# A two-block sequence model in float32 on one core: operands moved to one common place modulo 512 bytes, and the split weights of eight-tile units set 16, 32, 64 and 256 bytes into their buffers

## The chip, the core and the metric

The kernel runs on one core of a Trainium2 chip. The metric is device microseconds of one execution, as the median of several runs; lower is better. Engines are named as the profile names them: PE multiplies matrices and loads its weights (PEld), ACT, DVE and POOL work elementwise, SP issues the transfers from memory.

## The reference, cut to what matters

Two blocks over 512 frames of 1024 channels, float32. Every block is a chain of a normalisation, a wide projection, a mixer (delta rule and state space heads, then stick-breaking attention with pooling, then gated linear attention), a projection back, and a convolutional feed-forward layer of width 2816. What takes the time is the products of the activations with the weights:

```python
proj = h @ w_in                                  # 1024 x (mixer width)
mix = jnp.concatenate([o_a, o_s], axis=-1) @ w_out
u = causal_dwconv(h @ w_up, ffn_conv_w, ffn_conv_b)   # 1024 x 5632, three times
gate, up = jnp.split(u, 2, axis=-1)
f = (jax.nn.silu(gate) * up) @ w_down                 # 2816 x 1024, three times
```

Nothing of this arithmetic is touched by the change.

## The kernel before, in words

**Products.** Activations lie with channels on the 128 partitions and the 512 frames along a row, so a tile of activations is 128 x 512 words, 2048 bytes in every partition. A weight unit is one output tile of 128 channels: eight (or eleven, in the down projections) blocks of 128 x 128 words, 512 bytes each in every partition. Each product is made in fp32r, a faster matmul form, from a high and a low part of both operands: for each block k there are three matmuls, high weight by high activations, high weight by low activations, low weight by high activations (`multiply`, lines 253 to 255, 24 of them for a unit of eight tiles and 33 for one of eleven). `fan` (lines 229 to 231) does the same for the first two or three units of a stage side by side, and `mix_pe` (lines 2632 to 2634) for the first mixer's projection back. Every matmul has a weight load of its own, which the profile shows as PEld beside the matmul before it.

**Buffers.** SP loads a unit into one of four `raw` buffers (`load_units`). ACT writes the rounded high part to `whi[u % 2]` (`split_hi`, line 185) and DVE the rest to `wlo[u % 2]` (`split_lo`, line 191). Both wait for semaphores of the unit two places before. So units alternate between two pairs of buffers. `first_weights` (`first_hi`, `first_lo`) are two more pairs in the scratch region for the first two units of a stage, and `early` two for the first stage of all.

**Where things lie.** `fixed` hands out rows one behind the other, each rounded up to 32 bytes: `X`, `HH` and `HL` (the high and low part of the normalised activations, eight tiles each), four `raw`, two `whi`, two `wlo` (5632 bytes each), then `par` (914 columns of parameters), `cst` and `small`. Behind them, at the next multiple of `LINE` = 128 bytes, `FREE` begins, the scratch region, whose parts stand at multiples of 2048 bytes from `FREE`: the high and low parts that the feed-forward layer makes (`FH`, `FL`, 22 tiles each), those of the mixers' outputs (`DH`/`DL`, `MH`/`ML`, `PH`/`PL`), the `first` and `early` weights, and the mixers' own scratch. `TMP`, six more tiles, is counted from the end of the memory.

All rows up to `par` are multiples of 512 bytes long, and `X` is put at byte 16512, so `X`, `HH`, `HL`, `raw`, `whi` and `wlo` all begin at 128 modulo 512. `par` takes 3656 bytes, rounded up 3680, which is 7 x 512 + 96; `cst` and `small` are multiples of 512. So `FREE` falls on 224 rounded up to 256 modulo 512: everything in scratch stands 128 bytes on from everything in front of `par`, modulo 512. A block of weights is 512 bytes and a tile 2048, so within a buffer every block and every tile begins at the same place modulo 512 as the buffer.

**Order of the work.** The stages follow one another as in the reference; PE takes units in their order, `acc` alternates between two accumulators, and ACT, DVE and POOL handle a unit's results while PE is at the next ones. In the feed-forward layers PE runs 44 units of eight tiles on `HH`/`HL` (up) and then 16 units of eleven tiles on `FH`/`FL` (down), three times over. In the mixers, units are run in parts of six matmuls between the mixer's own small ones.

Of the kernel before, what the change touches and what calls it, by code (L numbers as in the profile page):

```python
# [25 lines left out]
P = 128  # L26
S = 512
D = 1024
KD = D // P
# [4 lines left out]
LINE = 128  # L34
RAW = 4
SPLIT = 2
# [3 lines left out]
def at(base, i, per):  # L40

    return base if i is None else base + per * i
# [22 lines left out]
def program(nc, x_in, w8, w11, par_in, cst_in, small_in, out, plan):  # L65
    cols = columns()
    ctx = ExitStack()
    with ctx:

        top = [(nc.sbuf_base + 31) // 32 * 32]  # L70

        def fixed(name, shape, dt=F32):
            t = nc.alloc_sbuf_tensor_at(name, shape, dt, offset=top[0])
            top[0] += (4 * shape[1] + 31) // 32 * 32
            return t

        X = fixed("X", [P, KD * S])
        base_h = top[0]
        HH = fixed("HH", [P, KD * S], F32R)
# [2 lines left out]
        raw = [fixed(f"raw{j}", [P, HALF * P]) for j in range(RAW)]  # L82
        whi = [fixed(f"whi{j}", [P, HALF * P], F32R) for j in range(SPLIT)]
        wlo = [fixed(f"wlo{j}", [P, HALF * P], F32R) for j in range(SPLIT)]
        par = fixed("par", [P, cols.n])
        cst = fixed("cst", [P, 15 * P])
        small = fixed("small", [P, small_in.shape[1]])
        FREE = (top[0] + LINE - 1) // LINE * LINE
        TMP = (nc.sbuf_usable_end - 6 * TILE) // LINE * LINE

        def place(name, n, offset, dt=F32):
            assert offset >= FREE and offset + 4 * n <= nc.sbuf_usable_end, name
            return nc.alloc_sbuf_tensor_at(name, [P, n], dt, offset=offset)
# [19 lines left out]

        sq = [place(f"sq{j}", S, TMP + j * TILE) for j in range(2)]
        hn = [place(f"hn{j}", S, TMP + (2 + j) * TILE) for j in range(2)]
        ln = place("ln", S, TMP + 4 * TILE)
        rs = place("rs", S, TMP + 5 * TILE)
        squares = place("squares", KD * S, FREE + 24 * TILE)
        taps = [place(f"taps{j}", S, TMP + j * TILE) for j in range(4)]
        FH = place("FH", KF * S, FREE, F32R)  # L120
        FL = place("FL", KF * S, FREE + KF * TILE, F32R)
        assert FREE + 2 * KF * TILE <= TMP
        first_weights = {}
        for at0 in (0, 8, 16):
            first_weights[at0] = [tuple(place(f"first_{n}{at0}_{j}", KD * P, FREE + (at0 + 4 * j + 2 * m) * TILE, F32R)
                                        for m, n in enumerate(("hi", "lo"))) for j in range(2)]
# [51 lines left out]

        def split_hi(act, u, i, per, kt, first=None, behind=SPLIT):

            hi = whi[u % SPLIT] if first is None else first[0]
            act.wait_ge(raw_in[u % RAW], at(16 * (u // RAW + 1), i, 16 * per // RAW))
            if u >= behind and first is None:
                act.wait_ge(unit_done, at(u - behind + 1, i, per))
            nc.scalar.activation(hi[:, 0:kt * P], raw[u % RAW][:, 0:kt * P], ACT.Copy).then_inc(w_hi_ready, 1)  # L185

        def split_lo(dve, u, i, per, kt, first=None, behind=SPLIT):

            hi, lo = (whi[u % SPLIT], wlo[u % SPLIT]) if first is None else first
            dve.wait_ge(w_hi_ready, at(u + 1, i, per))  # L190
            nc.vector.tensor_tensor(lo[:, 0:kt * P], raw[u % RAW][:, 0:kt * P],  # L191
                                    hi[:, 0:kt * P].bitcast(F32), ALU.subtract).then_inc(w_lo_ready, 1)
# [27 lines left out]
        def fan(pe, c, hi, lo, ready, after=None):  # L220

            u0, n = c["u"], c["fan"]
            w = [c["first"][j] if j < 2 else (whi[(u0 + j) % SPLIT], wlo[(u0 + j) % SPLIT]) for j in range(n)]
            pe.wait_ge(w_lo_ready, u0 + n)
            for k in range(KD):
                pe.wait_ge(ready[0], ready[1] + k + 1)
                for j in range(n):
                    a, (wh, wl) = c["spare"][j], (x[:, k * P:(k + 1) * P] for x in w[j])
                    nc.tensor.matmul(a[:, :], wh, tile(hi, k), start=k == 0, stop=False)  # L229
                    nc.tensor.matmul(a[:, :], wh, tile(lo, k), start=False, stop=False)  # L230
                    last = nc.tensor.matmul(a[:, :], wl, tile(hi, k), start=False, stop=k == KD - 1)  # L231
                    if k == KD - 1:
                        last.then_inc(unit_done, 1)
                if after and k in after:
                    after[k]()

        def multiply(pe, u, t, i, per, per_t, kt, hi, lo, start=True, stop=True, ready=None, part=None, c=None):

            w, a, m = u % SPLIT, acc[t % 2], None
            if c and u - c["u"] < len(c["spare"]) + 2:  # L240
                m = u - c["u"]
                a = accum(c, m)
            if not part:
                pe.wait_ge(w_lo_ready, at(u + 1, i, per))
                if m is not None:
                    pe.wait_ge(acc_read, c["t"])
                elif start and t >= 2:
                    pe.wait_ge(acc_read, at(t - 1, i, per_t))
            for k in range(kt) if part is None else range(kt * part // 4, kt * (part + 1) // 4):
                if ready:  # L250
                    pe.wait_ge(ready[0], ready[1] + k + 1)
                wh, wl = whi[w][:, k * P:(k + 1) * P], wlo[w][:, k * P:(k + 1) * P]
                nc.tensor.matmul(a[:, :], wh, tile(hi, k), start=start and k == 0, stop=False)  # L253
                nc.tensor.matmul(a[:, :], wh, tile(lo, k), start=False, stop=False)  # L254
                last = nc.tensor.matmul(a[:, :], wl, tile(hi, k), start=False, stop=stop and k == kt - 1)  # L255
            if part in (None, 3):
                last.then_inc(unit_done, 1)
# [23 lines left out]
        def norm_act(act, c, made):  # L281
            for k in range(KD):
                act.wait_ge(*made(k))
                square(act, c, tile(X, k), k, sq, hn[0])
            split_hi(act, 0, None, 0, KD, early[0])
# [8 lines left out]
        def norm_dve(dve, c, gain):  # L294
# [8 lines left out]
            for k in range(KD + 1):  # L303
                if k < KD:
                    nc.vector.scalar_tensor_tensor(out=tile(normed_x, k), in0=tile(X, k), scalar=col(gain[0], gain[1] + k),
                                                   in1=rs[:, :], op0=ALU.mult, op1=ALU.mult).then_inc(hn_ready, 1)
# [10 lines left out]
        def later_act(act, c, gain, made):  # L317
            for k in range(KD):
                act.wait_ge(*made(k))
                nc.scalar.activation(tile(HH, k), tile(X, k), ACT.Copy, scale=col(gain[0], gain[1] + k)).then_inc(hh_ready, 1)  # L320
                nc.scalar.activation(tile(squares, k), tile(X, k), ACT.Square).then_inc(sq_ready, 1)
            next_splits(split_hi, act, c["next"])
# [4 lines left out]
        def ahead_act(act, c, gain, made, k):  # L327
            act.wait_ge(*made(k))
            nc.scalar.activation(tile(HH, k), tile(X, k), ACT.Copy, scale=col(gain[0], gain[1] + k)).then_inc(hh_ready, 1)
            square(act, c, tile(X, k), k, sq, hn[0])  # L330

# [2289 lines left out]
        def mix_pe(pe, c):  # L2621
            for m, (k, h) in enumerate(MIX):
                u, w, a = c["u"] + m, (c["u"] + m) % SPLIT, mix_acc(c, k)
                pe.wait_ge(w_lo_ready, u + 1)
                if h == 0 and k not in (2, 3):
                    pe.wait_ge(acc_read, c["t"] + k - 1)
                hi, lo = ((DH, DL), (HH, HL))[h]
                for j in range(KD):
                    if m in (0, 4):
                        pe.wait_ge(h_ready, c["h"] - 2 * KD + h * KD + j + 1)  # L2630
                    wh, wl = whi[w][:, j * P:(j + 1) * P], wlo[w][:, j * P:(j + 1) * P]
                    nc.tensor.matmul(a[:, :], wh, tile(hi, j), start=h == 0 and j == 0, stop=False)  # L2632
                    nc.tensor.matmul(a[:, :], wh, tile(lo, j), start=False, stop=False)  # L2633
                    last = nc.tensor.matmul(a[:, :], wl, tile(hi, j), start=False, stop=h == 1 and j == KD - 1)  # L2634
                last.then_inc(unit_done, 1)
                if m == 1:
                    ssd_sums(pe, 1)
                if m == len(MIX) - 2:
                    squares_pe(pe, c, total1)
            last_square_pe(pe, c, sq1)  # L2640
# [36 lines left out]
        n = dict(next_first=None, u=-1, t=0, sq=0, rms=0, hn=0, h=0, ffn=0, pair=0, scaled=0, ssum=0, add=0, hh=0, tap=0, conv=0, x=0, w8=0, w11=0)  # L2677
# [4 lines left out]
        for at_, (kind, arg) in enumerate(plan):  # L2682
            c = dict(n)
# [293 lines left out]
```

## Time and profile before

| | |
|---|---|
| runs, us | 2166.68, 2168.47, 2169.84; median 2168.47 |
| profiled execution, first to last instruction | 2157.8 us (what its run took around that is not listed; the median of the runs is 10.7 us above it) |
| PE busy | 2109.7 us, 98% |
| PEld busy | 1698.0 us, 79% |
| DVE, ACT, POOL busy | 1213.1, 906.3, 325.6 us |
| granted clock of PE, mean | 0.998 |
| DMA | 88 GB/s in the mean |

The busy time of PE counts a matmul from its start to the modelled end of its pass through the array, and matmuls overlap, so the busy share says little about the rate. The rate is the distance from the start of one matmul to the start of the next.

### The profile page before, as it was taken

The numbers are of one execution on the slowest core, as the hardware profiler recorded it, in microseconds if no ns is written. First come the engines' busy times: TensorE is split into PE (matmuls) and PEld (weight loads), VectorE is DVE, ScalarE is ACT, GpSimd is POOL, SyncE is SP. The second block draws the span as 40 slices with busy tenths as digits, with TensorE's granted clock in tenths as the row PEclk, the third lists the DMA queues.
The fourth block names the chain that finished last, engine by engine and source line by source line (L and its number), as shares of the span: only waits on it lengthen the run. The fifth ranks groups of instructions, "written<-read, shape, count | busy, mean of one in ns | idle before, by whom it ended". The sixth has DMA issues, their size and how long they took to land.

```text
span 2157.8 us, 26841 instructions
## 1 busy us (share of the span) xinstructions
PE 2109.7 (98%) x9776; PEld 1698.0 (79%) x9776; DVE 1213.1 (56%) x1663; ACT 906.3 (42%) x1282; POOL 325.6 (15%) x266
## 2 busy tenths in 40 slices
PE   6999999999999999999999999999999999999999
PEld 5778888878868888877766888888878878888887
DVE  5898755765366665226544566653354465666522
ACT  6883445434254444224564444442242354444311
POOL 0002121220122222001302122210000011222100
PEclk9999999999999999999999999999999999999999
DMA  7323322122323233221111333232222122323321
GB/s 234 93 77 92 86 74 69 59 69 69 101 65 97 94 94 120 94 86 59 59 40 50 97 94 94 95 116 96 80 77 88 51 78 88 98 97 97 114 94 66
DMA packets 81481, 188.96 MB, mean 88 GB/s; under 512 B 19824, under 2 KB 40432, under 8 KB 81392
## 3 DMA queue, kind: packets, MB, share of 16 engines
q1 hardware_dynamic: 81392, 187.75, 27.6%
q8 instruction: 59, 0.97, 0.2%
q14 instruction: 30, 0.25, 0.0%
HBM read 178.28 MB, written 9.44 MB: 87 GB/s over the span
## 4 chain that ended last, share of the span: by engine, by line
PE 92%; DVE 4%; ACT 2%; issue 1%; DMA 0%; POOL 0%; SPq 0%; ACTq 0%; DVEq 0%; POOLq 0%
PE acc L253 23%; PE acc L255 23%; PE acc L254 23%; PE bank L1726 1%; PE bank L1245 1%; PE bank L229 1%; PE bank L230 1%; PE bank L231 1%; PE acc L2634 1%; PE acc L2633 1%; PE acc L2632 1%; PE bank L2017 1%; PE bank L253 1%; PE bank L255 1%; PE bank L254 1%
## 5 line engine op out<-in xcount | busy, mean ns | idle before, releaser
L253 PE MATMUL acc<-HH,whi 128*128 128x512 f32 x1600 | 642.1, 401 | 7.1 <-DVE wlo L191 4.5
L255 PE MATMUL acc<-HH,wlo 128*128 128x512 f32 x1600 | 624.4, 390 | 0.0
L254 PE MATMUL acc<-HL,whi 128*128 128x512 f32 x1600 | 623.5, 390 | 0.0
L185 ACT ACTIVATE whi<-raw 128x1024 fp32r<-128x1024 f32 (+1 forms) x293 | 324.2, 1108 | 573.5 <-PE acc L255 543.4
L191 DVE TENSOR_TENSOR wlo<-raw,whi 128x1024 fp32r<-128x1024 f32 (+1 forms) x293 | 400.9, 1369 | 287.8 <-ACT whi L185 287.8
L253 PEld LDWEIGHTS acc<-HH,whi 128*128 128x128 f32 x1600 | 301.1, 188 | 74.1 <-DVE wlo L191 11.0
L255 PEld LDWEIGHTS acc<-HH,wlo 128*128 128x128 f32 x1600 | 300.5, 188 | 64.0
L254 PEld LDWEIGHTS acc<-HL,whi 128*128 128x128 f32 x1600 | 301.1, 188 | 62.0 <-issue 4.1
L253 PE MATMUL acc<-FH,whi 128*128 128x512 f32 x528 | 208.9, 396 | 0.0
L255 PE MATMUL acc<-FH,wlo 128*128 128x512 f32 x528 | 208.6, 395 | 0.0
L254 PE MATMUL acc<-FL,whi 128*128 128x512 f32 x528 | 208.5, 395 | 0.0
L388 DVE TENSOR_TENSOR acc<-acc,rs 128x512 f32<-128x512 f32 x150 | 104.8, 699 | 174.8 <-PE acc L255 174.8
L480 POOL TENSOR_TENSOR taps<-taps,taps 128x512 f32<-128x512 f32 x66 | 85.5, 1295 | 507.1 <-DVE taps L466 451.3
L445 ACT ACTIVATE FH<-taps 128x512 f32 (+1 forms) x66 | 41.8, 633 | 199.1 <-POOL taps L480 199.1
L253 PEld LDWEIGHTS acc<-FH,whi 128*128 128x128 f32 x528 | 99.1, 188 | 24.2 <-issue 0.2
L254 PEld LDWEIGHTS acc<-FL,whi 128*128 128x128 f32 x528 | 99.1, 188 | 24.2 <-issue 0.2
L255 PEld LDWEIGHTS acc<-FH,wlo 128*128 128x128 f32 x528 | 99.1, 188 | 24.1
L343 POOL TENSOR_TENSOR hn<-hn,sq 128x512 f32<-128x512 f32 x24 | 36.8, 1532 | 418.6 <-ACT sq L336 418.6
L466 DVE SCALAR_TENSOR_TENSOR taps<-acc,par,taps 128x510 f32<-128x510 f32 x117 | 87.6, 749 | 14.7 <-DVE taps L462 0.5
L485 POOL TENSOR_TENSOR FL<-taps,FH 128x512 f32 (+1 forms) x66 | 85.6, 1297 | 59.9 <-ACT FH L445 59.9
L436 ACT ACTIVATE taps<-acc,par 128x512 f32<-128x512 f32 x117 | 89.1, 762 | 1.6 <-DVE acc L388 1.6
L462 DVE SCALAR_TENSOR_TENSOR taps<-acc,par,taps 128x511 f32<-128x511 f32 x117 | 86.7, 741 | 0.0
(394 smaller groups left out, 2673.1 us busy)
## 6 DMA issues: line engine op xcount, KB each, us to landing
raw<-w SPq DMA_DIRECT2D x257, 512.0 KB, 3.5
raw<-w SPq DMA_DIRECT2D x48, 704.0 KB, 4.0
X<-x SPq DMA_DIRECT2D x4, 512.0 KB, 5.2
x_dram<-small SPq DMA_DIRECT2D x8, 256.0 KB, 4.4
xt_dram<-small SPq DMA_DIRECT2D x8, 256.0 KB, 3.6
a_dram<-l_am SPq DMA_DIRECT2D x8, 256.0 KB, 3.7
l_xt<-xt_dram SPq DMA_DIRECT2D x8, 256.0 KB, 3.5
l_x<-x_dram SPq DMA_DIRECT2D x8, 256.0 KB, 3.3
```

The source lines that it names most:

```text
L185: nc.scalar.activation(hi[:, 0:kt * P], raw[u % RAW][:, 0:kt * P], ACT.Copy).then_inc(w_hi_ready, 1)
L191: nc.vector.tensor_tensor(lo[:, 0:kt * P], raw[u % RAW][:, 0:kt * P], hi[:, 0:kt * P].bitcast(F32), ALU.subtract).then_inc(w_lo_ready, 1)
L253: nc.tensor.matmul(a[:, :], wh, tile(hi, k), start=start and k == 0, stop=False)
L254: nc.tensor.matmul(a[:, :], wh, tile(lo, k), start=False, stop=False)
L255: last = nc.tensor.matmul(a[:, :], wl, tile(hi, k), start=False, stop=stop and k == kt - 1)
L388: nc.vector.tensor_tensor(a[:, :], a[:, :], rs[:, :], ALU.mult).then_inc(scaled, 1)
L436: nc.scalar.activation(taps[j][:, :], a[:, :], ACT.Identity, scale=w(2), bias=w(3)).then_inc(tap_ready, 1)
L445: nc.scalar.activation(o, taps[j - 1][:, :], ACT.Copy).then_inc(fh_ready, 1)
L462: nc.vector.scalar_tensor_tensor(out=taps[j][:, 1:S], in0=a[:, 0:S - 1], scalar=w(1), in1=taps[j][:, 1:S], op0=ALU.mult, op1=ALU.add).then ...
L466: nc.vector.scalar_tensor_tensor(out=taps[j][:, 2:S], in0=a[:, 0:S - 2], scalar=w(0), in1=taps[j][:, 2:S], op0=ALU.mult, op1=ALU.add).then ...
L480: nc.gpsimd.tensor_tensor(taps[2 * b][:, :], taps[2 * b][:, :], taps[2 * b + 1][:, :], ALU.mult).then_inc(prod_ready, 1)
L485: nc.gpsimd.tensor_tensor(o, taps[2 * b][:, :], h.bitcast(F32), ALU.subtract).then_inc(f_ready, 1)
```

## The change

`par` moves to the front, and what follows it is rounded up to a multiple of 128 bytes. All later rows are multiples of 512 bytes long, so `X`, `HH`, `HL`, `raw`, `whi`, `wlo`, `cst`, `small` and `FREE` now begin at the same place modulo 512 (an assertion says so of `FREE`). Further, a new helper `weights` gives the high and low part of a unit: for units of eleven tiles they begin at the start of the buffers, as before; for units of eight tiles they begin 4 words (16 bytes) into `whi[0]`, 8 words (32 bytes) into `wlo[0]`, 16 words (64 bytes) into `whi[1]` and 64 words (256 bytes) into `wlo[1]`. ACT's and DVE's splits write there, and `fan`, `multiply` and `mix_pe` read there. The `first` and `early` weights are not shifted. No instruction is added or removed, and no wait is changed.

```diff
+        par = fixed("par", [P, cols.n])
+        top[0] = (top[0] + LINE - 1) // LINE * LINE
         X = fixed("X", [P, KD * S])
...
-        par = fixed("par", [P, cols.n])
+        SHIFT = ((4, 8), (16, 64))
+
+        def weights(w, kt):
+
+            hi, lo = SHIFT[w] if kt == KD else (0, 0)
+            return whi[w][:, hi:hi + kt * P], wlo[w][:, lo:lo + kt * P]
+
         cst = fixed("cst", [P, 15 * P])
...
         FREE = (top[0] + LINE - 1) // LINE * LINE
+        assert (FREE - base_h) % S == 0
...
-            hi = whi[u % SPLIT] if first is None else first[0]
+            hi = weights(u % SPLIT, kt)[0] if first is None else first[0]
...
-            hi, lo = (whi[u % SPLIT], wlo[u % SPLIT]) if first is None else first
+            hi, lo = weights(u % SPLIT, kt) if first is None else first
...
-            w = [c["first"][j] if j < 2 else (whi[(u0 + j) % SPLIT], wlo[(u0 + j) % SPLIT]) for j in range(n)]
+            w = [c["first"][j] if j < 2 else weights((u0 + j) % SPLIT, KD) for j in range(n)]
...
-                wh, wl = whi[w][:, k * P:(k + 1) * P], wlo[w][:, k * P:(k + 1) * P]
+                wh, wl = (x[:, k * P:(k + 1) * P] for x in weights(w, kt))
...
-                    wh, wl = whi[w][:, j * P:(j + 1) * P], wlo[w][:, j * P:(j + 1) * P]
+                    wh, wl = (x[:, j * P:(j + 1) * P] for x in weights(w, KD))
```

## Rows read from the trace of the kernel before

**Rows 1.** The page: span and busy time of the engines.

```profile
span 2157.8 us, 26841 instructions
...
PE 2109.7 (98%) x9776; PEld 1698.0 (79%) x9776; DVE 1213.1 (56%) x1663; ACT 906.3 (42%) x1282; POOL 325.6 (15%) x266
```

**Rows 2.** The page: the chain that ended last, shares of the span by engine.

```profile
PE 92%; DVE 4%; ACT 2%; issue 1%; DMA 0%; POOL 0%; SPq 0%; ACTq 0%; DVEq 0%; POOLq 0%
```

**Rows 3.** Busy time by window, PE alone, up projections: stretch, length, busy (matmuls), clock, DMA.

```profile
660.00:840.00 180.00, 180.00 (x796) 1.00 0.31 99
1240.00:1450.00 210.00, 210.00 (x927) 1.00 0.32 102
```

**Rows 4.** The same view of stretches in two down projections.

```profile
895.00:955.00 60.00, 60.00 (x259) 1.00 0.27 87
1475.00:1565.00 90.00, 90.00 (x387) 1.00 0.26 85
```

**Rows 5.** Timeline of PE (start, length), fan of the second up stage, 33 matmuls.

```profile
1560.83 0.39 PE L229 MATMUL bank<-HH,first_hi 128*128 128x512 f32 x1
...
1568.30 0.39 PE L231 MATMUL bank<-HH,first_lo 128*128 128x512 f32 x1
```

**Rows 6.** Timeline of PE, last projection back: first and last of 43 matmuls.

```profile
1759.83 0.39 PE L253 MATMUL acc<-PH,whi 128*128 128x512 f32 x1
...
1769.59 0.39 PE L253 MATMUL acc<-PH,whi 128*128 128x512 f32 x1
```

**Rows 7.** Lines 218 and 254: matmul durations in ns, min/median/max.

```profile
L218 PE MATMUL bank<-first_hi x36: 387/389/792, 594.4 to 977.7; 128*128 128x512 f32 x36
...
L254 PE MATMUL acc<-HL,whi x1600: 387/389/628, 34.0 to 2030.9; 128*128 128x512 f32 x178
...
L254 PE MATMUL acc<-FL,whi x528: 387/392/404, 848.3 to 2154.0; 128*128 128x512 f32 x176
```

**Rows 8.** Timeline of PE while the granted clock is at its lower level.

```profile
1748.41 0.50 PE L253 MATMUL acc<-PH,whi 128*128 128x512 f32 x1 [2.73 <-DVE PL L764]
...
1749.79 0.63 PE L255 MATMUL acc<-PH,wlo 128*128 128x512 f32 x1
...
1752.35 0.63 PE L255 MATMUL acc<-PH,wlo 128*128 128x512 f32 x1
```

**Rows 9.** Timeline of PE, one part of a unit between small matmuls, first mixer.

```profile
194.77 0.39 PE L254 MATMUL acc<-HL,whi 128*128 128x512 f32 x1
...
195.93 0.38 PE L2084 MATMUL bank<-l_qd,l_small 128*128 128x128 f32 x2
```

**Rows 10.** Groups by line and shape, PE: count, busy us, mean ns, idle before.

```profile
L253 PE MATMUL acc<-HH,whi 128*128 128x512 f32 x1600 | 642.1, 401 | 7.1 <-DVE wlo L191 4.5 <-ACT l_z L1793 2.4
...
L253 PE MATMUL acc<-FH,whi 128*128 128x512 f32 x528 | 208.9, 396 | 0.0
...
L253 PE MATMUL bank<-HH,whi 128*128 128x512 f32 x88 | 36.5, 414 | 0.0
L229 PE MATMUL bank<-HH,first_hi 128*128 128x512 f32 x80 | 34.4, 429 | 1.0 <-DVE HL L361 1.0
...
L253 PE MATMUL acc<-MH,whi 128*128 128x512 f32 x64 | 26.1, 408 | 1.6 <-DVE wlo L191 1.1 <-POOL ML L1182 0.5
...
L253 PE MATMUL acc<-PH,whi 128*128 128x512 f32 x64 | 25.9, 405 | 2.7 <-DVE PL L764 2.7
...
L2632 PE MATMUL acc<-HH,whi 128*128 128x512 f32 x48 | 19.1, 398 | 0.0
L2632 PE MATMUL acc<-DH,whi 128*128 128x512 f32 x48 | 19.0, 396 | 0.0
...
L2632 PE MATMUL bank<-DH,whi 128*128 128x512 f32 x16 | 6.7, 419 | 0.0
```

**Rows 11.** The same view, ACT: the high parts of units of eight tiles.

```profile
L185 ACT ACTIVATE whi<-raw 128x1024 fp32r<-128x1024 f32 x245 | 257.9, 1054 | 371.7 <-PE acc L255 341.6 <-PE acc L2634 12.4 <-PE bank L231 8.7
```

**Rows 12.** The same view, DVE: the low parts of units of eight tiles.

```profile
L191 DVE TENSOR_TENSOR wlo<-raw,whi 128x1024 fp32r<-128x1024 f32 x245 | 322.9, 1319 | 155.6 <-ACT whi L185 155.6
```

## The prediction, made before the changed kernel was run

> **What bounds the kernel now.** The page comes first: PE is busy for 98% of the span, DVE for 56%, ACT for 42% [rows 1], and the chain that ended last runs through PE for 92% of its length and through DMA for none [rows 2]. So PE's rate sets the time almost everywhere, and whatever changes the distance between two matmuls is paid in full. Busy time doesn't show that distance, since matmuls overlap; I read it from how many fit into a stretch. The view of busy time by window counts every matmul that runs in it, so also the one that began up to 0.39 us (its length) ahead. In two up projections that is 180.39 us / 796 = 226.6 ns and 210.39 / 927 = 227.0 ns [rows 3]; I use 226.7. In two down projections it is 60.39 / 259 = 233.2 ns and 90.39 / 387 = 233.6 ns [rows 4]; I use 233.4. Both stretches are filled by matmuls of one shape, at the full granted clock, with no idle time.
>
> Why do the down projections go 6.7 ns slower? In the up projections weights (`whi`, `wlo`) and activations (`HH`, `HL`) begin at the same place modulo 512. In the down projections the activations (`FH`, `FL`) stand 128 bytes further than the weights. Two other pairs tell whether that is it or something in the down projections. In a fan, `HH` meets weights of the scratch region, so that now the weights stand 128 bytes further: 32 matmuls lie between the starts of the two rows, 7.47 us / 32 = 233.4 ns [rows 5]. In the last projection back `PH` meets `whi` and `wlo`: 42 matmuls in 9.76 us, 232.4 ns [rows 6]. And where line 218 multiplies scratch by scratch, the median duration is 389 ns, as for `HL` by `whi`, where `FL` by `whi` has 392 [rows 7]. So neither the region nor the stage decides, but whether both operands stand at the same place. Also, the extra time isn't a fixed price of a matmul: while the granted clock is at its lower level of 1.2 GHz, after PE had sat idle for 2.73 us, six matmuls of the 128-byte pair take 2.56 us, 426.7 ns each, which is 512 columns at 1.2 GHz with nothing on top [rows 8]. At 2.4 GHz 512 columns would be 213.3 ns, so the same place costs 13.4 ns on top and 128 bytes apart 20.1 ns.
>
> **The change, part by part.** A matmul's own weights are loaded while the one before runs, so the distance that counts is between a running tile and the next block of weights.
>
> (a) `FH` and `FL` come to the place of the unshifted weights: 528 x 3 = 1584 matmuls [rows 10] by 233.4 - 226.7 = 6.7 ns, 10.6 us off.
>
> (b) `first` weights come to the place of `HH` and are not shifted: 80 x 3 = 240 matmuls [rows 10] by 6.7 ns, 1.6 us off.
>
> (c) The units of eight tiles on `HH` and `HL` lose the common place that they had: (1600 + 88 + 48) x 3 = 5208 matmuls [rows 10]. The trace has no row of 16, 32, 64 or 256 bytes. Bounds: from below, all of the 13.4 ns goes, since at 512 columns and 2.4 GHz nothing is left to gain; from above, the nearest slower row is 233.4 ns, 6.7 ns more. I take the straight line between the two distances that have rows, 6.7 / 128 = 0.052 ns a byte: 0.8 ns for 16 bytes, 1.7 for 32, 3.4 for 64. For 256 bytes I take nothing: +128 and -128 cost the same [rows 4, 5], and those are one place only if the pattern repeats every 256 bytes. Two of every three loads are of the high part, so units in the first pair of buffers pay (2 x 0.8 + 1.7) / 3 = 1.1 ns and those in the second (2 x 3.4 + 0) / 3 = 2.3 ns, 1.7 in the mean: 5208 x 1.7 = 8.9 us on.
>
> (d) `DH`, `MH`, `PH` and their low parts go from 128 bytes to the shifts: (48 + 16 + 64 + 64) x 3 = 576 matmuls [rows 10] by 6.7 - 1.7 = 5.0 ns, 2.9 us off.
>
> (e) ACT's and DVE's splits write at shifted addresses. They take 1054 and 1319 ns and have 371.7 us of PE-made idle time and 155.6 us of ACT-made idle time ahead of them [rows 11, 12]: that idle time hides a longer split, and I cost it at nothing. Were the cover gone, the end of it would show where PE waits for `wlo`, 4.5 us in all in the largest group [rows 10]; a fifth longer there would be 1 us. Moving `par` changes no issue and no queue.
>
> Sum: -10.6 - 1.6 + 8.9 - 2.9 = -6.2 us. Against the profiled span that is 2157.8 to 2151.6; the median of the runs stands 10.7 us above that span, for what lies around it, and goes to 2162. Not all of (c) is settled at 226.7 today: in the short parts between a mixer's small matmuls five distances at the common place took 1.16 us, 232 ns each [rows 9], so the place is not all that counts there. The first mixer has 53 units, 1272 matmuls; if they feel nothing of the shift, (c) is 2.2 us cheaper.
>
> **The rivals.** With x for the mean price of the shifts per matmul, the whole is -12.2 - 3.9 + 5.78 x us (5784 matmuls of units of eight tiles); it turns from gain to loss at x = 2.8 ns.
>
> *The shift breaks what the common place gave* (slower). The up projections hold 226.7 ns over hundreds of matmuls [rows 3], while at the same place short parts run at 232 [rows 9]. So 226.7 may be a state that the stream falls into and keeps, and every unit now changes the distance, twice within itself. Then all units of eight tiles run as `FH` does today: x = 6.7, +22.7 us, 2191. For it: no stretch in which the operands stand apart goes under 232.4 [rows 4 to 6]. Against: 16 and 32 bytes are small beside 128. It shows first in the up projections, and decides from a period of 229.5 ns on. Chance 0.36, with everything past x = 3.5.
>
> *The shift pays.* If the common place is itself a collision of the two reads, a few bytes could part them. Half of the 13.4 ns regained, x = -6.7, is -54.9 us: 2114. For it: the 13.4 ns are there to be had [rows 3, 8]. Against: no stretch shown goes under 226.6. Chance 0.12.
>
> *The place does nothing*, and what parts 226.7 from 233.4 is something else, or gains and losses cancel: 2168. Against: rows 5 to 7 exchange stage and region and keep the 6.7 ns. The Trainium skill, TensorE: Matmul & The Clock Gate, section "Step-by-step: what each phase is for", says that PE reads moving tiles and weights through two independent ports and that loading the next weights takes nothing from the running matmul; by that rule the change is worth 0 and the time stays at 2168. The two periods, 226.7 and 233.4 ns for one shape, do not agree with it. Chance 0.1.
>
> **How the numbers follow.** A measurement of this kernel tells 0.2%, 4.3 us, from no change. My forecast, the line between the rows with x from about -1 to 3, has 0.42; its own range is 2146 to 2170, its middle 2162. Of it 0.35 lie below x = 2.0, where the gain passes 4.3 us. Faster: 0.35 + 0.12 = 0.47; within 0.2%: 0.07 + 0.1 = 0.17; slower: 0.36. The range reaches to just past the slower rival at 2191, and a third of the way to the gain at full rate: 2136 to 2193.
>
> **What would show it.** In the profile after: down projections at 226.7 ns and `FL` by `whi` at a median of 389 (part a); fans of `first` weights at 226.7 (b); in the up projections alternate units of different period, the first pair of buffers near 227.8 and the second near 229.0 (c); DMA, ACT and DVE as they are (e). The forecast is wrong if the up projections run at 231 or more, or under 226, and its ground is wrong if the down projections stay at 233.

## The result, and the profile after

| | before | after |
|---|---|---|
| median of the runs, us | 2166.83 (6 runs, 2158.72 to 2169.84) | 2177.49 (6 runs, 2176.16 to 2178.87) |
| ratio, with its 95% interval | | 1.0058 [1.0040, 1.0076] |

The changed kernel is slower by 10.7 us in the medians, 12.6 us by the ratio. Its profiled execution took 2178.87 us for a span of 2177.1, so 1.8 us lie around a span, and not the 10.7 us that the prediction put there: the rest goes with the granted clock. The span is 19.3 us above that of [rows 1], more than the medians differ, because the profiled execution of before was one of the quicker ones (mean granted clock 0.998, after it 0.995): its trace has the clock at the lower level for 10 us of the span, the trace after for 24 us. So I take sizes from medians and ratios, and from the traces only what doesn't depend on that: the distance between matmuls inside a stage at full clock.

The medians still mix executions of different clock. Of those that have 0.997, the kernel before took 2161.0 to 2161.8 us (four, among those measured beside the experiments), the changed one 2176.2 (one): at the same clock the change costs about 15 us.

The page of the kernel after, its span, its engines and the chain that ended last (compare [rows 1, 2]):

```profile
span 2177.1 us, 26841 instructions
...
PE 2131.1 (98%) x9776; PEld 1705.2 (78%) x9776; DVE 1212.1 (56%) x1663; ACT 905.7 (42%) x1282; POOL 325.6 (15%) x266
...
PE 91%; DVE 5%; ACT 2%; issue 1%; DMA 0%; POOL 0%; DVEq 0%; ACTq 0%
```

The same instructions ran, with the same engine in charge. DVE, ACT and POOL are as busy as before to 1 us; only PE has more to do.

Busy time by window for PE of the kernel after, two up projections and one down projection (stretch, length, busy with the count of matmuls, clock, DMA share, GB/s; compare [rows 3, 4]):

```profile
660.00:840.00 180.00, 180.00 (x773) 1.00 0.29 93
1240.00:1450.00 210.00, 210.00 (x902) 1.00 0.31 99
900.00:950.00 50.00, 50.00 (x222) 1.00 0.27 94
```

Counted as in the prediction (the stretch and 0.39 us, over the count) the up projections now run at 180.39 / 773 = 233.4 ns and 210.39 / 902 = 233.2 ns, where they had 226.7, and the down projection at 50.39 / 222 = 227.0 ns, where it had 233.4. The two kinds of stage have changed places, and there are about twice as many matmuls in the slower kind.

Timeline of PE of the kernel after, in the first up projection (start, length): two starts with 27 distances between them, a whole unit of eight tiles and the beginning of the next, from the other pair of buffers:

```profile
694.96 0.40 PE L262 MATMUL acc<-HH,whi 128*128 128x512 f32 x1
...
701.26 0.40 PE L262 MATMUL acc<-HH,whi 128*128 128x512 f32 x1
...
1574.97 0.39 PE L238 MATMUL bank<-HH,first_hi 128*128 128x512 f32 x1
...
1579.73 0.39 PE L238 MATMUL bank<-HH,first_hi 128*128 128x512 f32 x1
```

6.30 / 27 = 233.3 ns across both pairs: the pair with 16 and 32 bytes isn't cheaper than the one with 64 and 256 (over the whole projection, unit by unit, 233.4 and 233.3). The last two rows are a fan of unshifted `first` weights, 21 distances in 4.76 us, 226.7 ns, where it had 233.4 [rows 5]. (In both kernels this fan opens the third mixer, not an up stage: it follows the second down projection.)

Line 263 (it was 254) of the kernel after, durations of its matmuls in ns as min/median/max (compare [rows 7]):

```profile
L263 PE MATMUL acc<-HL,whi x1600: 387/394/628, 32.9 to 2053.6; 128*128 128x512 f32 x178
L263 PE MATMUL acc<-FL,whi x528: 389/389/398, 863.9 to 2173.3; 128*128 128x512 f32 x176
...
L263 PE MATMUL acc<-ML,whi x64: 390/394/398, 1142.3 to 1207.0; 128*128 128x512 f32 x64
```

Groups by line and shape of the kernel after; lines 262, 194 and 200 were 253, 185 and 191 (busy us, mean ns, idle before; compare [rows 10 to 12]):

```profile
L262 PE MATMUL acc<-HH,whi 128*128 128x512 f32 x1600 | 653.8, 409 | 6.4 <-DVE wlo L200 3.9 <-ACT l_z L1802 2.3
...
L194 ACT ACTIVATE whi<-raw 128x1024 fp32r<-128x1024 f32 x245 | 257.7, 1053 | 394.2 <-PE acc L264 363.9 <-PE acc L2643 12.4 <-PE bank L240 8.7
L200 DVE TENSOR_TENSOR wlo<-raw,whi 128x1024 fp32r<-128x1024 f32 x245 | 322.9, 1319 | 147.9 <-ACT whi L194 147.9
```

`HL` by `whi` went from a median of 389 to 394 ns and `FL` by `whi` from 392 to 389. The splits take 1053 and 1319 ns, as before, and PE waits 3.9 us for `wlo` where it waited 4.5.

### The profile page after: what moved, and what is told of

Same layout as the page of the kernel before. It is cut to its first block, busy times and chain, and to the rows that moved or that the text cites. A ratio compares the mean times of both kernels' runs of the same rounds, so it can differ in the third digit from the quotient of the medians.

```text
span 2177.1 us, 26841 instructions
## 1 busy us (share of the span) xinstructions
PE 2131.1 (98%) x9776; PEld 1705.2 (78%) x9776; DVE 1212.1 (56%) x1663; ACT 905.7 (42%) x1282; POOL 325.6 (15%) x266
## 3 DMA queue, kind: packets, MB, share of 16 engines
q1 hardware_dynamic: 81392, 187.75, 27.1%
## 4 chain that ended last, share of the span: by engine, by line
PE 91%; DVE 5%; ACT 2%; issue 1%; DMA 0%; POOL 0%; DVEq 0%; ACTq 0%
PE acc L262 23%; PE acc L264 23%; PE acc L263 23%; PE bank L1254 1%; PE bank L238 1%; PE acc L2641 1%; PE acc L2643 1%; PE acc L2642 1%; PE bank L239 1%; PE bank L240 1%; PE bank L1735 1%; PE bank L2026 1%; DVE wlo L200 1%; PE bank L262 1%; PE bank L264 1%
## 5 line engine op out<-in xcount | busy, mean ns | idle before, releaser
L262 PE MATMUL acc<-HH,whi 128*128 128x512 f32 x1600 | 653.8, 409 | 6.4 <-DVE wlo L200 3.9
L264 PE MATMUL acc<-HH,wlo 128*128 128x512 f32 x1600 | 633.9, 396 | 0.0
L263 PE MATMUL acc<-HL,whi 128*128 128x512 f32 x1600 | 631.6, 395 | 0.0
```

## The experiments

Two theories stood against each other. **The line:** a distance between activations and weights costs in proportion to its bytes, up to 128. **The step:** any distance, however small, puts the stream into the slower period of 233 ns. Each run below also tells whether the two halves of the change, the moved rows and the shifts, add up.

In the runs called scans the rows lie as in the changed kernel, and each of the three up projections has shifts of its own, alike for the high and the low part unless it is said; all units elsewhere have none. Units alternate between two pairs of buffers, so one projection tells two distances. "Per unit" is the distance from the first matmul of a unit to the first of the next, over 24.

**1. The moved rows alone (align_only).** No shifts.

```diff
-        SHIFT = ((4, 8), (16, 64))
+        SHIFT = ((0, 0), (0, 0))
```

> The changed kernel with all four shifts at zero, so that every pair of weights and activations stands at one place modulo 512. All theories: units of eight tiles go back to 226.7 ns a matmul, the down projections stay at the 226.7 ns that they have after the change. Step theory (the shifts alone cost, 6.7 ns on each of the matmuls of the eight-tile units): the gains (a), (b) and (d) of the prediction remain, 12.2 + 3.9 = 16 us under the kernel before, near 2151 of 2167, ratio 0.9925. If the time were only 6 us under it, the gains were overrated by more than half; if not under it at all, the alignment buys nothing that the end sees.

Measured: 2147.96 us (2145.25 to 2153.03, 6 runs), before beside it 2167.26; ratio 0.991 [0.9895, 0.9924]. Windows of PE in this kernel:

```profile
660.00:840.00 180.00, 180.00 (x796) 1.00 0.30 98
1240.00:1450.00 210.00, 210.00 (x928) 1.00 0.32 101
900.00:950.00 50.00, 50.00 (x222) 1.00 0.27 85
```

Up and down projections alike run at 226.6 to 227.0 ns now. By the medians the moved rows gain 19.3 us, and the shifts cost 2177.5 - 2148.0 = 29.5 us, which is more than the whole loss of the change. At a mean granted clock of 0.997 three executions took 2145.3 to 2145.7 us, against 2161.0 to 2161.8 before: 15.8 us gained, and 30.7 lost by the shifts. So this kernel is quicker than both of the case.

**2. Equal shifts (scan_a).** The stage is looked up from the unit's number; the other scans change `SHIFT` alone. In words of 4 bytes, (high, low) of the first pair and of the second, for the three up projections:

```diff
-        SHIFT = ((4, 8), (16, 64))
+        SHIFT = (((4, 4), (8, 8)), ((16, 16), (32, 32)), ((64, 64), (48, 48)))
+        up_units = []
...
-        def weights(w, kt):
+        def weights(u, kt):
...
-            hi, lo = SHIFT[w] if kt == KD else (0, 0)
+            w = u % SPLIT
+            stage = [k for k, u0 in enumerate(up_units) if u0 <= u < u0 + 2 * KF]
+            hi, lo = SHIFT[stage[0]][w] if kt == KD and stage else (0, 0)
```

> High and low part of a unit shifted alike, other distances in each up projection, first and second pair of buffers: 16 and 32 bytes in the first, 64 and 128 in the second, 256 and 192 in the third; all other units unshifted. Line theory (the prediction's): 227.5 and 228.4 ns a matmul in the first, 230.0 and 233.4 in the second, 226.7 and 230.0 in the third. Step theory (every distance but a multiple of 256 bytes costs the same): 233.3 in the whole first and second, 226.7 in the units of 256 bytes. Mixture theory (it is only the change of the distance from load to load within a unit that costs): 226.7 in all but perhaps 128.

Measured: 2166.68 us. Windows of PE in three up projections:

```profile
660.00:840.00 180.00, 180.00 (x774) 1.00 0.30 94
1240.00:1450.00 210.00, 210.00 (x904) 1.00 0.31 100
1860.00:2020.00 160.00, 160.00 (x705) 1.00 0.31 96
```

That is 233.1 ns (16 and 32 bytes), 232.7 (64 and 128) and 227.5 (256 and 192). Per unit: 16 bytes 233.3, 32 bytes 232.8, 64 bytes 232.9, 128 bytes 232.4. The line asks for 227.5 at 16 bytes. The third projection holds two kinds of unit, as the timeline of PE shows, by the starts of a unit of 192 bytes, of one of 256, and of the next:

```profile
1921.58 0.39 PE L265 MATMUL acc<-HH,whi 128*128 128x512 f32 x1
...
1927.07 0.39 PE L265 MATMUL acc<-HH,whi 128*128 128x512 f32 x1
...
1932.51 0.39 PE L265 MATMUL acc<-HH,whi 128*128 128x512 f32 x1
```

5.49 / 24 = 228.8 ns at 192 bytes, 5.44 / 24 = 226.7 at 256. So 256 bytes is free, as the prediction took it, and the shifts from 16 to 128 bytes cost nearly the whole step. 192 bytes fits neither theory: the line asks for 230.0, the step for 233.3.

**3. Still smaller and larger shifts (scan_b).**

```diff
+        SHIFT = (((1, 1), (2, 2)), ((24, 24), (56, 56)), ((128, 128), (96, 96)))
```

> As the scan before it, with 4 and 8 bytes in the first up projection, 96 and 224 in the second, 512 and 384 in the third. Line theory: 226.9 and 227.1; 231.7 and 228.4 (32 bytes from 256); 226.7 and 233.4. Step theory: 233.3 in all but the units of 512 bytes, with 4 and 8 bytes open, since they stay within 16 bytes. If the pattern repeats every 512 bytes and not every 256, then 256 bytes cost something in the scan before and 512 nothing here. A stretch under 226.6 in either scan would speak for distances that pay.

Measured: 2167.64 us. Windows of PE, the same three stretches:

```profile
660.00:840.00 180.00, 180.00 (x779) 1.00 0.30 94
1240.00:1450.00 210.00, 210.00 (x901) 1.00 0.31 99
1860.00:2020.00 160.00, 160.00 (x697) 1.00 0.29 94
```

Per unit: 4 bytes 232.4, 8 bytes 231.0, 96 bytes 233.7, 224 bytes 233.3, 512 bytes 227.4, 384 bytes 232.9. One word of shift costs 5.7 of the 6.7 ns. And 384 bytes costs what 128 does while 512 is nearly free: the pattern repeats every 256 bytes.

**4. High and low part apart (scan_c).** One part shifted and the other not, then both off by distances that differ by 256 bytes; both pairs alike.

```diff
+        SHIFT = (((0, 16), (0, 16)), ((16, 0), (16, 0)), ((4, 68), (4, 68)))
```

> High and low parts at different distances, the same in both pairs of buffers: first up projection 0 for the high and 64 bytes for the low part, second 64 and 0, third 16 and 272. Line theory: a third, then two thirds of the price of 64 bytes (227.8 and 228.9 ns), third 227.5. Step theory with a price for every load off the common place: 228.9 with a third of the loads off it, 231.1 with two thirds, 233.3 with all. Mixture theory: the first two cost most, whatever the share, and the third, with 16 bytes for all loads modulo 256, costs nothing.

Measured: 2162.84 us. Windows of PE, the same three stretches:

```profile
660.00:840.00 180.00, 180.00 (x781) 1.00 0.30 95
1240.00:1450.00 210.00, 210.00 (x903) 1.00 0.31 100
1860.00:2020.00 160.00, 160.00 (x687) 1.00 0.29 94
```

That is 231.0 ns with only the low part 64 bytes off, 233.0 with only the high part, 233.5 with 16 and 272 bytes. Two of three loads are of the high part. One load off its place in three already costs 4.3 of the 6.7 ns, where a price per load would ask for a third of it, 2.2: the price belongs to the stream, not to the single load.

The third stretch begins too late to show the most telling thing of this run. Here are two windows of PE that cover the third projection from its start on, and the timeline between them:

```profile
1820.70:1858.60 37.90, 37.90 (x169) 1.00 0.32 100
1859.00:2037.00 178.00, 178.00 (x764) 1.00 0.30 98
```

```profile
1858.77 0.44 PE L265 MATMUL acc<-HH,whi 128*128 128x512 f32 x1
1859.05 0.39 PE L266 MATMUL acc<-HL,whi 128*128 128x512 f32 x1
```

With the same 16 and 272 bytes, seven units run at 38.29 / 169 = 226.6 ns. Then one distance is 0.28 us long, and from there to the end of the projection the pace is 178.39 / 764 = 233.5 ns. The kernel of the first experiment, without shifts, has a long distance (0.27 us) at the same unit, and comes back to its pace:

```profile
1816.00:1853.90 37.90, 37.90 (x169) 1.00 0.33 99
1856.20:2028.00 171.80, 171.80 (x759) 1.00 0.31 100
```

```profile
1854.05 0.44 PE L262 MATMUL acc<-HH,whi 128*128 128x512 f32 x1
1854.32 0.40 PE L263 MATMUL acc<-HL,whi 128*128 128x512 f32 x1
```

It has 226.6 ns ahead of it and 172.19 / 759 = 226.9 from nine matmuls behind it on. So one distance can hold either period. At the common place the stream came back after the disturbance, at 16 bytes modulo 256 it did not. The step theory is too simple in this, and the mixture theory, which expected no price here, was right for seven units.

**5. Shifts in whole multiples of 256 bytes (far_shift).** The split weights stand 256 and 256 bytes into the first pair, 512 and 768 into the second, in all units of eight tiles.

```diff
-        SHIFT = ((4, 8), (16, 64))
+        SHIFT = ((64, 64), (128, 192))
```

> All four buffers shifted, but by 256, 256, 512 and 768 bytes, the rest as changed. Step theory (only the place modulo 256 bytes counts): no price at all, 226.7 ns a matmul in the up projections, the time of the kernel with no shift, near 2148 (ratio 0.991 to the kernel before). If shifting as such costs (other addresses for the splits of ACT and DVE, other strides from buffer to buffer), or if the pattern is 512 bytes long, it is above 2155.

Measured: 2151.66 us (2150.80 to 2152.76, 4 runs), before beside it 2166.68; ratio 0.994 [0.9919, 0.9961]. Windows of PE:

```profile
660.00:840.00 180.00, 180.00 (x796) 1.00 0.31 98
1240.00:1450.00 210.00, 210.00 (x929) 1.00 0.32 102
```

226.6 and 226.5 ns, as without shifts. So shifting as such, the other addresses that ACT and DVE write and the places that PE reads, costs nothing to speak of; what costs is the place modulo 256. The median is 3.7 us above that of the first experiment, but all four executions had a clock of 0.993 (2150.8 to 2152.8 us), and the two of the first experiment at 0.993 took 2151.6 and 2153.0. That ACT and DVE write off the common place isn't what costs either: they did so throughout the seven units of the fourth experiment at 226.6 ns.

**6. Only one pair shifted (half_shift).**

```diff
-        SHIFT = ((4, 8), (16, 64))
+        SHIFT = ((4, 8), (0, 0))
```

> The changed kernel with the second pair of buffers unshifted, the first at 16 and 32 bytes. Step theory, with a stream that falls back into 226.7 ns within a unit: the units of the first pair at 233.3, those of the second at 227 to 228; half of the 29.5 us that lie between the changed kernel and the one without shifts, 2161 to 2165. If an unsettled stream stays unsettled, units of both pairs are near 233 and the time is near 2175. Line theory: 16 and 32 bytes are a third of the whole price, 2158.

Measured: 2164.28 us (2158.54 to 2170.32, 10 runs); ratio to before 0.9994 [0.9979, 1.0009]. A window of PE in the second up projection, then its timeline in the third: the start of an unshifted unit, of its tenth matmul, of the next (shifted) unit, and of the one after that:

```profile
1240.00:1450.00 210.00, 210.00 (x913) 1.00 0.31 100
```

```profile
1879.50 0.40 PE L262 MATMUL acc<-HH,whi 128*128 128x512 f32 x1
...
1881.58 0.39 PE L262 MATMUL acc<-HH,whi 128*128 128x512 f32 x1
...
1884.97 0.39 PE L262 MATMUL acc<-HH,whi 128*128 128x512 f32 x1
...
1890.56 0.40 PE L262 MATMUL acc<-HH,whi 128*128 128x512 f32 x1
```

The unshifted unit begins at 2.08 / 9 = 231.1 ns and goes on at 3.39 / 15 = 226.0, which is 226.7 within the rounding of the starts; the shifted one takes 5.59 / 24 = 232.9. A unit's pace follows its own place, but not at once: an unshifted unit needs some nine matmuls to come back to the quicker period. So half of the shifts lose somewhat more than half: 210.39 / 913 = 230.4 ns is 3.7 of the 6.7. The ratios agree (of the 1.48% between the first experiment's and the change's, 0.84%), but with intervals of 0.15% either way they wouldn't tell it from half. The time lies in the 2161 to 2165 expected of a stream that falls back within a unit.

**7. The shifts alone (shift_only).** The row order of before, with the change's shifts.

```diff
-        par = fixed("par", [P, cols.n])
-        top[0] = (top[0] + LINE - 1) // LINE * LINE
         X = fixed("X", [P, KD * S])
...
+        par = fixed("par", [P, cols.n])
         cst = fixed("cst", [P, 15 * P])
```

> The kernel before with the shifts alone, its rows where they were. Step theory: the matmuls on HH and HL go from 226.7 to 233.3 ns, as in the changed kernel, those on FH and FL stay at 233.4, those on the mixers' scratch stay near 233: the whole loss and none of the gain, 2167 + 29 = 2196, at most 2202 (5208 x 6.7 ns = 35 us). Line theory: 2176.

Measured: 2188.09 us (2185.44 to 2189.01, 4 runs); ratio 1.0107 [1.0085, 1.0130]. Windows of PE:

```profile
660.00:840.00 180.00, 180.00 (x773) 1.00 0.30 95
1240.00:1450.00 210.00, 210.00 (x902) 1.00 0.30 97
900.00:950.00 50.00, 50.00 (x216) 1.00 0.26 87
```

Up and down projections are both at 233.3 ns here. The shifts alone cost 21.4 us by the medians, 23.2 by the ratio; over the 5208 matmuls that leave their common place that is 4.1 to 4.5 ns each, and the sign of the change without its moved rows is beyond doubt. The step theory's 2196 is missed by 8 us: it charged every matmul the whole 6.7 ns, which the mixers don't pay (below). The halves add up only roughly: 29.5 us for the shifts behind the moved rows, less the 3.9 us of part (d), which the shifts alone can't undo, is 25.6, against these 21.4 to 23.2; what makes the difference stays open.

**8. Distances between 48 and 240 bytes (scan_d).**

```diff
+        SHIFT = (((60, 60), (52, 52)), ((44, 44), (40, 40)), ((36, 36), (12, 12)))
```

> Last scan of distances, high and low part alike, first and second pair of buffers: 240 and 208 bytes in the first up projection, 176 and 160 in the second, 144 and 48 in the third. Step theory: all between 231 and 234 ns, as 4 to 128 bytes were; distances short of 256 may be a little cheaper, as 192 bytes was (228.9). Collision theory (some place pays): a stretch under 226.6 ns somewhere; with none here, no distance in steps of 16 bytes up to 256 but 80 and 112 would be left for it.

Measured: 2162.37 us. Per unit: 240 bytes 227.8, 208 bytes 231.9, 176 bytes 230.3, 160 bytes 233.9, 48 bytes 233.1, and, against the rest, 144 bytes 226.9. Timeline of PE, third up projection, starts of a unit of 144 bytes, of one of 48, and of the next of 144:

```profile
1877.56 0.39 PE L265 MATMUL acc<-HH,whi 128*128 128x512 f32 x1
...
1883.00 0.40 PE L265 MATMUL acc<-HH,whi 128*128 128x512 f32 x1
...
1888.60 0.39 PE L265 MATMUL acc<-HH,whi 128*128 128x512 f32 x1
```

5.44 / 24 = 226.7 ns and 5.60 / 24 = 233.3. So some distances other than multiples of 256 reach the quicker period, but none tried goes under it.

**9. Two of these again, throughout a stage (scan_e).** 144 bytes in both pairs, 240 in both, and 80 and 112.

```diff
+        SHIFT = (((36, 36), (36, 36)), ((60, 60), (60, 60)), ((20, 20), (28, 28)))
```

> One distance for both pairs of buffers: 144 bytes in the first up projection and 240 in the second, the two distances between 0 and 256 at which units of the scan before held 226.7 ns; 80 and 112 bytes in the third, which no scan had. If the two are places of their own that hold the fast period, the first two stages run at 226.7 ns throughout, with no dearer matmul at the units' edges. If those units were only carried by their neighbours, they run at 231 to 234. For 80 and 112 bytes 231 to 234 is expected; under 226.6 would be a place that pays.

Measured: 2164.04 us. Windows of PE, the same three stretches as in the other scans:

```profile
660.00:840.00 180.00, 180.00 (x773) 1.00 0.30 95
1240.00:1450.00 210.00, 210.00 (x922) 1.00 0.32 101
1860.00:2020.00 160.00, 160.00 (x689) 1.00 0.30 96
```

144 bytes throughout runs at 233.4 ns, though it ran at 226.7 beside units of 48 bytes; 240 throughout runs at 228.2; 80 and 112 at 232.8. So the distance alone doesn't settle the period, as the third projection of the fourth experiment has shown already: what ran before a unit counts too. (The stage of 144 bytes alone began at the lower clock; whether it would hold 226.7 ns if it began at that pace wasn't tried.) The paces "per unit" of the scans hold beside the neighbours that they were measured with.

## Why the prediction was wrong

**What bounds the kernel: right.** PE's rate is the time. The matmul distances of the stages account for the direction of every run, and the other engines' busy times stayed.

**Parts (a) and (b): right.** Down projections came to 227.0 ns and the fans to 226.7, as forecast. With the shifts taken out, the moved rows gained 15.8 us at equal clock; the prediction's own formula at x = 0 has 16.1. The medians of the two kernels without any shift modulo 256 bytes lie on either side (19.3 us in the first experiment, 15.0 in the fifth).

**Part (c): the step that failed.** "I take the straight line between the two distances that have rows, 6.7 / 128 = 0.052 ns a byte". There is no line. Sixteen bytes cost 6.6 ns where the line has 0.8, 64 bytes 6.2 where it has 3.4, and 4 bytes 5.7; in the changed kernel both pairs of buffers run at 233.3 ns, where (c) had 227.8 and 229.0. What stands in its place is two periods, 226.7 and 233.3 ns: off the common place the stream can lose the quicker one at a single long distance and not come back (fourth experiment). The row that spoke against the line was there: [rows 3, 4] have two periods and nothing between, and [rows 9] show 232 ns at the common place itself, in short parts. Both say that 226.7 is something that the stream keeps only under conditions. The prediction saw this, and put it under its slower rival; as likeliest it took the interpolation, with nothing to show that the quantity is smooth.

**The size of it.** The whole change is 22.9 us worse than the -12.2 of (a) and (b), so -3.9 + 5.78 x = 22.9, and x = 4.6 ns a matmul; by the ratio (12.6 + 12.2 = 24.8) 5.0; at equal clock (14.9 + 12.2 = 27.1) 5.4. The forecast had 1.7 and the slower rival 6.7. In the up projections the rival is exact: 42 shifted units x 24 x 3 = 3024 matmuls by 6.7 ns are 20.3 us of the 29.5 that the shifts cost. The others, in the mixers and the projections back, bear the remaining 9.2 us: 2856 of them, 3.2 ns each (the count in (c) left out 96, two more groups of sixteen blocks, `bank<-HH,whi` at lines 229 and 2632; 0.2 us at its own price). The traces place them. From the last matmul of the first down projection to the first of the fan behind the second mixer, in the changed kernel and in the first experiment's:

```profile
984.04 0.39 PE L264 MATMUL acc<-FH,wlo 128*128 128x512 f32 x1
1207.42 0.39 PE L238 MATMUL bank<-HH,first_hi 128*128 128x512 f32 x1
...
975.19 0.39 PE L264 MATMUL acc<-FH,wlo 128*128 128x512 f32 x1
1196.35 0.39 PE L238 MATMUL bank<-HH,first_hi 128*128 128x512 f32 x1
```

223.4 us against 221.2, at the full clock throughout: 2.2 us over 528 shifted matmuls, 4.2 ns each. The stretch from the start to the fan behind the first mixer's projection back took 614.4 against 611.7 us, with 20 us at the lower clock in both: 2.7 us over 1593, 1.7 ns each. That its price is small fits [rows 9]: parts of six matmuls are over before the nine that an unshifted unit needed in the sixth experiment to settle. Over their last four distances the parts of six there (71 in each trace at the full clock) have a median of 231.5 ns without shifts and 232.3 with them, so there was little to lose; its units of 24 in a row go from 231.4 to 236.8.

**256 bytes at nothing: right** (226.7 ns in the second experiment, no loss in the fifth). The high part of that pair stood 64 bytes off, and the fourth experiment shows why a free low part then saves nothing: with only the high part off, 233.0 ns.

**Part (d): wrong with (c).** `ML` by `whi` has a median of 394 ns, no better than the 392 of a 128-byte pair [rows 7], since one off-place distance was exchanged for another of the same price. The 2.9 us were not there.

**Part (e): right.** The splits kept their durations to 1 ns, and the fifth experiment shifts them without a loss.

**The rivals.** *The shift breaks what the common place gave* is what happened, with its own sign shown by stage as it asked: up projections past 229.5 ns. Its 2191 is too high by the mixers' smaller price. *The shift pays* falls: of the distances tried, none held units under 226.6 ns, so none of them regained any of the 13.4 ns above 512 columns. *The place does nothing* falls by the first experiment: one kernel ran 29.5 us apart from the other with every instruction the same and only the weights' place different. The Trainium skill, TensorE: Matmul & The Clock Gate, section "Step-by-step: what each phase is for", says that loading the next weights takes no read bandwidth from the running matmul. The runs don't agree with what the prediction took from that rule, that the place is worth nothing. Whether it is read bandwidth that the slower period lacks, they don't show.

## What to carry to other kernels

Where matmuls follow one another without idle time, let streamed tiles and weights begin at the same place modulo 256 bytes: moving and padding one row gained 0.7 to 0.9% here, and no instruction changed. Between two measured points don't interpolate a price that may be a step: when the rows show two levels and nothing between, give the step the larger chance. And read the rate from matmuls per stretch, stage by stage, since the busy share of PE stood at 98% in both kernels.

## What the runs showed of the hardware that was not expected

All of this is for 512 columns in fp32r at the full clock, in streams of 24 matmuls and more.

- One word of distance is enough: 4 bytes cost 5.7 ns of a 226.7 ns matmul, where most distances up to 224 bytes cost 3.6 to 7.2, and the pattern repeats at 256 (256, 512 and 768 bytes together 226.6 ns, 128 and 384 bytes 232.4 and 232.9).
- The stream has a memory. At 16 bytes modulo 256 it held 226.6 ns for seven units and 233.5 for the rest of the stage, with one distance of 0.28 us between; without a shift it came back from such a distance. 144 bytes ran at 226.7 ns between units of 48 bytes and at 233.4 in a stage of its own; an unshifted unit behind a shifted one took some nine matmuls to come back.
- 192 and 240 bytes lie between the two levels (228.8, and 227.8 to 228.2 ns), while 64 and 16 bytes, their complements to 256, don't (232.9 and 233.3). That may mean that the price depends on which of the two operands stands further; it isn't shown, since they had other neighbours.

What in the reading of the two operands makes these two periods was not settled; it shows only at the full clock, since at 1.2 GHz a 128-byte pair ran at 426.7 ns with nothing on top [rows 8].
